# Strassen-like FFN products: the sums of activations move to the middle of the following pair

## What is computed

```
def swiglu_ffn(h, w_up, w_down):
    gate, up = jnp.split(h @ w_up, 2, axis=-1)
    return (jax.nn.silu(gate) * up) @ w_down
...
D_FF = ((8 * D_MODEL // 3 + 127) // 128) * 128
...
x = x + FFN_RESIDUAL_SCALE * swiglu_ffn(h, w_ffn1_up[l], w_ffn1_down[l])
```

## Time and profile before

| | |
|---|---|
| Runs, three | 2237.89, 2242.66, 2243.89 us; median 2242.66 |
| The profiled execution | 2246.15 us, of which the span is 2244.4 |
| PE busy | 2178.8 us, 97% of the span |
| DVE, ACT, POOL busy | 1702.1, 947.4, 625.2 us |
| Granted TensorE clock, mean | 0.991 of full speed |
| First FFN, pairs and down projection | to about 680 us |
| Second FFN, pairs | from about 1600 to 2025 us, then its down projection |

### The profile page before, as it was taken

The page is one execution under the profiler, slowest core; times in us unless marked ns, Lnnn a source line. Parts: engine busy times, 40 slices in busy tenths (PEclk is TensorE's granted clock), DMA queues, the critical chain, the costliest instruction groups (busy, mean ns, idle before and its releaser), DMA issues.

```text
span 2244.4 us, 31503 instructions
## 1 busy us (share of the span) xinstructions
PE 2178.8 (97%) x10238; PEld 1794.4 (80%) x10238; DVE 1702.1 (76%) x2123; ACT 947.4 (42%) x1551; POOL 625.2 (28%) x714
## 2 busy tenths in 40 slices
PE   7999999999999999999999999999989999999997
PEld 6788877878788888888887888888867788888886
DVE  5877878878955999999998659364688876765557
ACT  5455555534455122222224225044355555554444
POOL 2887668999800000000000420000036600000000
PEclk9999999999999999999999999999999999999999
DMA  5235785469874344444544632553258733337764
GB/s 170 78 112 180 255 267 178 154 233 301 267 234 133 100 137 148 147 135 144 151 124 146 209 96 80 187 206 104 75 174 273 265 126 98 112 114 252 234 188 169
DMA packets 306625, 379.07 MB, mean 169 GB/s; under 512 B 27257, under 2 KB 199377, under 8 KB 306416
## 3 DMA queue, kind: packets, MB, share of 16 engines
q1 hardware_dynamic: 286576, 306.01, 43.0%
q0 software_dynamic: 18800, 67.85, 8.8%
q10 hardware_dynamic: 1168, 4.20, 0.5%
HBM read 256.06 MB, written 119.55 MB: 167 GB/s over the span
## 4 chain that ended last, share of the span: by engine, by line
PE 77%; DVE 14%; issue 3%; ACT 3%; DMA 2%; SPq 0%; DVEq 0%; ACTq 0%
PE PU L1392 9%; PE PU L1394 9%; PE PU L1332 9%; PE PU L1393 9%; PE PU L1333 8%; PE PU L1334 8%; PE PD L1267 3%; PE PD L1268 3%; PE PD L1269 3%; PE PU L1267 2%; PE PU L1268 2%; PE PU L1269 2%; DVE Alo L2060 2%; DVE Dlo L2057 2%; PE PD L1468 1%
## 5 line engine op out<-in xcount | busy, mean ns | idle before, releaser
L1332 PE MATMUL PU<-Hhi,Whi 128*128 128x512 f32 x896 | 352.8, 394 | 2.8 <-DVE Hlo L2479 2.7
L1333 PE MATMUL PU<-Hlo,Whi 128*128 128x512 f32 x896 | 349.5, 390 | 0.0
L1334 PE MATMUL PU<-Hhi,Wlo 128*128 128x512 f32 x896 | 349.4, 390 | 0.0
L2458 DVE SCALAR_TENSOR_TENSOR XT<-XT,wq 128x1024 f32<-128x1024 f32 x240 | 313.3, 1306 | 8.2
L1332 PEld LDWEIGHTS PU<-Hhi,Whi 128*128 128x128 f32 x896 | 168.6, 188 | 41.3 <-DVE Hlo L2479 4.0
L1334 PEld LDWEIGHTS PU<-Hhi,Wlo 128*128 128x128 f32 x896 | 168.6, 188 | 35.4
L1333 PEld LDWEIGHTS PU<-Hlo,Whi 128*128 128x128 f32 x896 | 168.5, 188 | 34.8 <-issue 0.7
L1392 PE MATMUL PU<-Hhi,Dhi 128*128 128x512 f32 x480 | 187.0, 389 | 2.2 <-ACT s1b L1734 2.2
L1394 PE MATMUL PU<-Hhi,Dlo 128*128 128x512 f32 x480 | 186.7, 389 | 0.0
L1393 PE MATMUL PU<-Hlo,Dhi 128*128 128x512 f32 x480 | 186.7, 389 | 0.0
L1267 PE MATMUL PD<-Dhi,Ahi 128*128 128x512 f32 x352 | 139.4, 396 | 7.1 <-DVE Alo L2060 7.1
(11 more groups left out here) (400 smaller groups left out, 5195.5 us busy)
## 6 DMA issues: line engine op xcount, KB each, us to landing
TAB<-in_w_ffn_down POOLq DMA_DIRECT2D x44, 512.0 KB, 5.3
d_sb<-TAB POOLq DMA_DIRECT2D x44, 512.0 KB, 4.3
Wraw<-in_w_ffn_up SPq DMA_DIRECT2D x80, 256.0 KB, 4.3
XT<-in_w_ffn_up SPq DMA_DIRECT2D x80, 256.0 KB, 4.0
d_sa<-XT SPq DMA_DIRECT2D x80, 256.0 KB, 2.4
Wraw<-in_w_in SPq DMA_DIRECT2D x32, 512.0 KB, 5.1
d_act<-G SPq DMA_DIRECT2D x48, 256.0 KB, 2.1
WRd<-d_sb SPq DMA_DIRECT2D x44, 256.0 KB, 3.4
```

Source lines behind the costliest of these rows:

```text
L1332: mm(o_, Whi[s][:, side, k, :], Hhi[:, k, hs[h]], start=k == 0, stop=False)
L1333: mm(o_, Whi[s][:, side, k, :], Hlo[:, k, hs[h]], start=False, stop=False)
L1334: last = mm(o_, Wlo[s][:, side, k, :], Hhi[:, k, hs[h]], start=False, stop=k == KT - 1)
L2458: stt(CVb, z_, w_, CVb, ALU.mult, ALU.add).then_inc(m["conv"], 1)
```

## The change

All four halves of a couple now lie in the kept blocks: `K2` and `K3` take the places of `E1` and `E2`, and the odd pair writes ACT1 to K2 and ACT2 to K3. S3 is made in K3 in the middle of the odd pair (before ACT2 goes there), and S1, S2 and S4 in the middle of the even pair that follows, in place: K1, K0, K2. Stores and waits follow: S3 is stored in the odd pair, the other three in the even one behind it, and the product that writes K3 waits for the landing of the store of S3. `comb_s16` and `silu_1` no longer wait for stores of G. Behind the last pair the three sums stand at the steps 4, 5 and 6 of the down projection.

```diff
-    K0, K1, E1, E2 = [XT[:, 6 + i // 2, (i % 2) * HW:(i % 2 + 1) * HW] for i in range(4)]
+    K0, K1, K2, K3 = [XT[:, 6 + i // 2, (i % 2) * HW:(i % 2 + 1) * HW] for i in range(4)]
...
         def store_pair(S, r):
 
             if second(r):
+                store_sums(S, r, (M_S3,))
                 store_kept(S, r, 1)
                 store_kept(S, r, 0)
                 store_sums(S, r, (M_S1, M_S2, M_S4))
             else:
                 store_kept(S, r, 0)
-                store_sums(S, r, (M_S3,))
...
         def comb_s16(S, r, saved1):
             q = pair_at(S, r)[0]
             dve.wait_ge(u_prod, q * 7 + POS[6])
             dve.wait_ge(u_s1, q + 1)
-            if second(r):
+            if isinstance(r, int) and r == 0:
+                dve.wait_ge(act_saved[1], saved1[1] + 32)
+            else:
                 dve.wait_ge(u_c, q * 7 + (C_ACT2 - 7))
-            else:
-                first = isinstance(r, int) and r == 0
-                dve.wait_ge(act_saved[1], saved1[1] + 32 if first else couple(S, r)[0] * 32 + saved1[1])
-                if not first:
-                    dve.wait_ge(u_sum, couple(S, r)[1] * 4)
...
             if second(r):
-                tt(s16b, s16b, s5b, ALU.mult).then_inc(u_c, 1)
-                return
-            dve.wait_ge(t_lo, 4 * (UBASE[S] // NSP) + 4)
-            if S is FFN2 or not isinstance(r, int) or r:
-                dve.wait_ge(sa_st, couple(S, r)[1] * 64)
-            tt(K1, s16b, s5b, ALU.mult).then_inc(u_c, 1)
+                dve.wait_ge(sa_st, couple(S, r)[1] * 64 + 16)
+            else:
+                dve.wait_ge(t_lo, 4 * (UBASE[S] // NSP) + 4)
+                if S is FFN2 or not isinstance(r, int) or r:
+                    dve.wait_ge(sa_st, couple(S, r)[1] * 64)
+            tt(K3 if second(r) else K1, s16b, s5b, ALU.mult).then_inc(u_c, 1)
...
-            tt(g1b if second(r) else K0, g1b, s167b, ALU.mult).then_inc(u_c, 1)
+            tt(K2 if second(r) else K0, g1b, s167b, ALU.mult).then_inc(u_c, 1)
...
+        def sum_3(S, r, saved):
+
+            q, (c, n) = pair_at(S, r)[0], couple(S, r)
+            dve.wait_ge(u_c, q * 7 + (C_ACT1 - 7))
+            dve.wait_ge(act_saved[1], c * 32 + saved[1])
+            tt(K3, K0, K1, ALU.subtract).then_inc(u_sum, 1)
...
+            tt(K1, K1, K3, ALU.add).then_inc(u_sum, 1)
...
+            tt(K0, K1, K0, ALU.subtract).then_inc(u_sum, 1)
...
+            dve.wait_ge(act_saved[1], c * 32 + (saved[1] + 32))
+            tt(K2, K2, K0, ALU.subtract).then_inc(u_sum, 1)
...
                 comb_s16(S, r, saved)
                 lo_w(S, coming, 6)
+                if second(r):
+                    sum_3(S, r, saved)
+                else:
+                    sum_1(S, after(r, -1))
                 comb_12(S, r)
+                if not second(r):
+                    sum_2(S, after(r, -1), saved)
                 lo_w(S, coming, 3)
+                if not second(r):
+                    sum_4(S, after(r, -1), saved)
                 comb_s167(S, r)
                 comb_22(S, r)
                 lo_w(S, coming, 7)
-                if second(r):
-                    sums_high(S, r)
                 comb_21(S, r)
                 lo_w(S, coming, 4)
-                if second(r):
-                    sum_low(S, r, saved)
-                else:
-                    sum_even(S, r)
```

More of the change, by code:

```diff
@@ L524, in store_kept @@
                          else d_act[bass.ds(number(f), 1)].rearrange("a p n -> (a p) n")[:, hs[h]],
-                         G[h][:, :] if second(r) else K0).then_inc(act_saved[second(r)], 16)
+                         (K3 if h else K2) if second(r) else K0).then_inc(act_saved[second(r)], 16)
         def store_sums(S, r, which):
@@ L599, in down @@
                 sp.wait_ge(u_lo, 7 * (UBASE[FFN2] + NSP - 1))
+            r = NSP - 1
             for t in range(RING):
                 load_product(S, 0, t)
-            r = NSP - 1
-            stores = {6: lambda: store_kept(S, r, 1), 7: lambda: store_kept(S, r, 0),
-                      8: lambda: store_sums(S, r, (M_S1, M_S2)), 10: lambda: store_sums(S, r, (M_S4,))}
+            store_sums(S, r, (M_S3,))
+            stores = {(0, 6): lambda: store_kept(S, r, 1), (0, 7): lambda: store_kept(S, r, 0),
+                      (0, 10): lambda: store_sums(S, r, (M_S1, M_S2)), (1, 1): lambda: store_sums(S, r, (M_S4,))}
             for p in range(7):
@@ L608, in down @@
                         load_product(S, p, t)
-                    if p == 0 and t in stores:
-                        stores[t]()
+                    if (p, t) in stores:
+                        stores[p, t]()
                     if (p, t) in D_ROWS_AT:
@@ L1750, in silu_1 @@
             act.wait_ge(u_prod, q * 7 + POS[2])
-            if second(r):
-                act.wait_ge(u_c, q * 7 + (C_ACT1 - 7))
-            elif isinstance(r, int) and r == 0:
+            if isinstance(r, int) and r == 0:
                 act.wait_ge(act_saved[0], saved0[0] + 32)
             else:
-                act.wait_ge(act_saved[1], couple(S, r)[0] * 32 + saved0[1])
-                act.wait_ge(u_sum, couple(S, r)[1] * 4)
+                act.wait_ge(u_c, q * 7 + (C_ACT1 - 7))
             fn(g1b, PUf[0][:, :], ACT.Silu).then_inc(u_g1, 1)
@@ L2287, in comb_21, with sum_1 @@
             dve.wait_ge(u_c, q * 7 + C_21)
-            tt(g1b if second(r) else K0, g1b, s167b, ALU.mult).then_inc(u_c, 1)
[L2290 to L2296, removed]
+            tt(K2 if second(r) else K0, g1b, s167b, ALU.mult).then_inc(u_c, 1)
[4 more added lines that the diff above has]
+            tt(K3, K0, K1, ALU.subtract).then_inc(u_sum, 1)
+        def sum_1(S, r):
             q, n = pair_at(S, r)[0], couple(S, r)[1]
@@ L2300, in sums_high, with sum_2, sum_4 @@
             dve.wait_ge(u_c, q * 7 + C_ACT2)
-            tt(K1, K1, G[1][:, :], ALU.add).then_inc(u_sum, 1)
+            tt(K1, K1, K3, ALU.add).then_inc(u_sum, 1)
+        def sum_2(S, r, saved):
+            c, n = couple(S, r)
             dve.wait_ge(u_sum, n * 4 + M_S1)
-            tt(E2, K1, K0, ALU.subtract).then_inc(u_sum, 1)
-        def sum_low(S, r, saved):
+            dve.wait_ge(act_saved[0], c * 16 + (saved[0] + 32))
+            tt(K0, K1, K0, ALU.subtract).then_inc(u_sum, 1)
+        def sum_4(S, r, saved):
             q, (c, n) = pair_at(S, r)[0], couple(S, r)
@@ L2369, in fast_ffn @@
             lo_w(S, 1, 4)
-            sum_even(S, 0)
             def body(r):
@@ L2426, in _ @@
         fast_ffn(FFN1, 0, 0, SAVED0[FFN1], "nf1")
-        down(FFN1, {(0, 5): lambda: sum_low(FFN1, NSP - 1, SAVED0[FFN1]), (3, 9): lambda: split_pair(R_MIX, 0), (5, 9): lambda: row_scale("nmx", 0),
+        down(FFN1, {(0, 4): lambda: sum_1(FFN1, NSP - 1), (0, 5): lambda: sum_2(FFN1, NSP - 1, SAVED0[FFN1]),
+                    (0, 6): lambda: sum_4(FFN1, NSP - 1, SAVED0[FFN1]), (3, 9): lambda: split_pair(R_MIX, 0), (5, 9): lambda: row_scale("nmx", 0),
                     (6, 9): lambda: turned("nmx", 0, 0), (6, 10): lambda: turned("nmx", 0, 1)})
@@ L2659, in _ @@
         fast_ffn(FFN2, R_FFN2, N1 + 2 * KT, SAVED0[FFN2], "nf2")
-        down(FFN2, {(0, 5): lambda: sum_low(FFN2, NSP - 1, SAVED0[FFN2]), (5, 8): fin_scale, (5, 10): fin_early, (6, 8): fin_half})
+        down(FFN2, {(0, 4): lambda: sum_1(FFN2, NSP - 1), (0, 5): lambda: sum_2(FFN2, NSP - 1, SAVED0[FFN2]),
+                    (0, 6): lambda: sum_4(FFN2, NSP - 1, SAVED0[FFN2]), (5, 8): fin_scale, (5, 10): fin_early, (6, 8): fin_half})
         fin_late()
```

10 lines of the change are left out of this document (4 added, 6 removed).

## The result

| | Before | Changed |
|---|---|---|
| Median, range | 2242.69, 2237.89 to 2243.89 us (4 runs) | 2268.12, 2261.45 to 2276.59 us (4 runs) |
| Profiled execution | 2246.15 us | 2276.59 us, span 2274.8 |

The ratio is 1.0119, 95% interval 1.0080 to 1.0159: slower by 25 us where 12 were forecast. The sign and the range (2226 to 2276) held; the size was half of what came. The profiled execution of the changed kernel is the slowest of its four, 8 us above their median.

A forecast was written before the change was run, and what follows sets the result against it. PE is busy 97% of the span, and in the busy FFN stretches waits only for comb_s16. Terms -24.1, -1.4, -1, +34.8 and +4 sum to +12.3 us: 2255.0 us against the median 2242.66, range 2226 to 2276.

The forecast's parts named there:

- Bound by comb_s16: In both busy FFN stretches PE waits only for comb_s16 to read PU01 before product 7: 8.5 and 6.6 us.
- even stalls from the late sums: All seven even-pair waits come from sums late in DVE's backlog and go when these move: -24.1 us.
- Pair 1, -1.4: Pair 1 of each FFN loses one 0.69 us operation ahead of a late comb_s16: -1.4 us, bounds 0 and -4.
- Junction, -1: At the change to the down projection, sums move within one DVE backlog: -1 us, bounds -3 and +3.
- Quiet couples, 0: In couples without busy POOL traffic, DVE's margin covers the later loads and the K1 wait: 0 us.
- First wait, the loads, 5.8 us in six pairs: Raw-block loads behind the sums' stores land 8.0 us into six busy odd pairs: 5.8 us each, +34.8 together.
- Second wait, "it costs nothing more": Even pair's product into K1 waits for the couple's stores; busy, it ends before the loads land, adding 0 us.
- +4 together: Odd pairs 7, 15 and 17 of FFN1, with POOL computing but few transfers, lose 0 to 4 us each, +4 together.
- Rival 3: Pile-up: last load 2.8 us later, hold_s5 behind the weights' split, 11 us lost in three pairs: 2271, chance 0.18.
- The Trainium skill's price: Store and load price, about 2.0 us fixed plus bytes at 436 GB/s; both waits would end 4 to 5 us earlier.

The follow-up runs named there:

- e4: The kernel before with sum 3 alone, and its store, moved to the middle of the odd pair: 2232.9 us, ratio 0.9964.
- e12: The changed kernel run again without any edit: 2266.6 us, ratio 1.0115.
- e9: The kernel before with one added wait in SP's queue that holds back the loads of the even pair's raw blocks: 2259.8 us, ratio 1.0096.
- e1: The changed kernel with the loads of the even pair's raw blocks ahead of the stores of sums 1, 2 and 4 in SP's queue: 2260.0 us, ratio 1.0093.
- e8: The changed kernel with POOL's loads and stores of the down weights cut to 16 columns, result not valid: 2244.1 us.
- e7: The changed kernel with POOL's subtractions on the down weights cut to 16 of 512 columns, result not valid: 2242.6 us.
- e2: The changed kernel with sum 1 written to K3, the wait for stores moved from the product into K1 to that into K0: 2273.3 us, ratio 1.0108.
- e6: The changed kernel with loads ahead of the sums' stores, sum 1 in K3, and sums 1, 2 and 4 stored one by one: 2218.7 us, ratio 0.9908.

## Why the prediction was right, and what it mis-sized

- **Bound by comb_s16, even stalls from the late sums:** right. Even pairs kept 3.8 of 24.1 us. The forecast of none from pair 8 on was not met: pair 8 of FFN1 lost 1.8, and pair 6 of FFN2 1.9, both behind an odd pair that was itself late.
- **Pair 1, -1.4:** undersized; -5.1, and e4 shows it is sum 3's doing. The stated reason (an operation of 0.69 ahead of a late comb_s16) does not give 2.2 and 2.9 us; I costed the operation and not the slower clock and the chain behind it, though by how much each counts no run tells.
- **Junction, -1:** the 0.0 is luck. PE idles 2.9 us at FFN1's down projection's splits, where it was 4.3, but 3.5 us for comb_s16 of pair 19 (below), and the 156th matmul behind that pair's copy comes 4.3 us later than before. 3.2 of it come back further on in this projection, and the part behind the last copy of FFN2 is 1.9 shorter. In e12 the same matmul comes 5.4 us earlier than before. The term is neither borne out nor refuted.
- **Quiet couples, 0:** right, 38.08 us, the wait on line 2275 of 2.17 us included.
- **First wait, the loads, 5.8 us in six pairs:** the mechanism is there, and its price from the landing on held (e9, and the 4.8 to 6.7 us above). The landing was mis-sized: the last load landed 6.2 to 13.0 us into the six pairs, 9.7 on average, where 8.0 was forecast. The transfers are not what was off (the last load took 7.3 us on average, as in the earlier trace rows); sum 4 was. It ended 14.4 to 19.3 us into the even pair, 16.6 on average, where 14.3 was forecast. This is the term that was most mis-sized, and it feeds both waits: the late landing alone is 1.7 of the 2.5 us by which comb_s16 came later than forecast.
- **Second wait, "it costs nothing more": wrong as a price.** It took a K1 wait that ends 1.1 us into the odd pair, from stores that land in 4.7 us, and the same sum 4 at 14.3. The stores took up to 7.6 us, and the kernel before already had one of 7.1 in this stretch, outside the one couple of the earlier trace rows. In the six pairs the wait ended 0.7 to 7.3 us in, 3.2 on average, and comb_s16 followed 11 to 14 us behind its end, where the prediction's own terms (last split done at 5.4, one split, then its 4.2) give about 9. By itself, with the loads early, this wait cost 30.8 us in the six pairs (e1); beside late loads it was the last to end in one of the six. Together: comb_s16 at 15.9 in place of 13.4, and 7.7 in place of 5.8 us lost.
- **Six couples priced as if each stood alone, and "+4 together" for pairs 7, 15 and 17:** wrong in the same way. A late odd pair starts the next even one with DVE behind, its sums end later, and the next odd pair is later still: 5.5, 8.6 and 5.0, 9.1, 11.4 in a row. Where comb_s16 of the even pair was late, sum 4 ended at 15.7 to 19.3, otherwise at 14.4 to 15.9. Pairs 7, 15 and 17 lost 10.9. Pair 19 lost PE 3.48 us in a way that no term had: line 2275 of pair 18 waited 4.27 us, so the K0 half was stored only at 480.00, and behind that store in SP's queue stand the down projection's first loads, for which ACT, and then DVE's split step ahead of comb_s16, waited. SP, ACT:

```profile
480.00 0.34 SPq L523 DMA_DIRECT2D d_act<-XT  x1
480.39 0.43 SPq L487 DMA_DIRECT2D WRd<-in_w_ffn_down  x1
```

```profile
484.40 0.63 ACT L1625 ACTIVATE Dhi<-WRd 128x512 fp32r<-128x512 f32 x1 [5.21 <-DMA WRd<-in_w_ffn_down]
```

- **Rival 3 (hold_s5 behind the split, 2271)** came nearest in size. Its mechanism cost PE 10.9 us of idling in all, against 32.9 for comb_s16 in the two stretches; in pair 9 of FFN1 the K1 wait feeds it, in pair 5 of FFN2 the late load, as the rival had it (ACT's split at 8.7 us).
- **The Trainium skill's price,** "DMA: Bandwidth & Descriptors", "Anatomy of one DMA", about 2.6 us by an estimate for 256 KB: in e8, with POOL's traffic nearly gone, the stores of FFN2's stretch took 2.0 to 3.0, and the trace agrees with it; in the changed kernel they took up to 7.6. The section is about transfers that GpSimd issues, and its sum of a fixed part and the bytes has no term for other traffic; these are SP's. The prediction's "4 to 5 us earlier" by that price fits the loads alone; the K1 wait would end some 2 us earlier (4.7 less 2.6).
- **DVE's slow sums.** Sums 1, 2 and 4 took 5.5 us in pair 8 against 2.07 in a quiet pair. The Trainium skill says in "GPSIMD Engine Reference", "Specifications", that GpSimd shares its SBUF interfaces with VectorE, with contention for DVE instructions that have two SBUF inputs. The traces agree: operations with a PSUM operand stayed at 0.67 in the same pair, and the sums took 0.69 in FFN2's stretch of e7, where POOL's subtractions were cut to 16 columns, against 1.5 on average in the changed kernel. Three such sums between comb_s16 and comb_s167 are exposed to it as they were at the odd pair's end.

## What to carry to other kernels

When work is moved off a late chain, list everything that is released by it at its new place, and lay the new waits beside each other: two of nearly equal height hide each other, so neither is "nothing more", and an experiment that eases one alone shows little (e1 gave 8 us and e2 nothing, both together 34). Ask the chain of waits which one ended last before naming a cause, pair by pair: here the largest total of waiting was not it. Price a wait in a busy stretch by the spread over the whole stretch, not by one couple, and let a late pair start the next one late. What is worth moving may be one piece of the change (e4), and a store should start when its own data are ready, with loads that wait for nothing ahead of it in the queue (e6).

## What was not expected of the hardware

Three 256 KB stores issued within 1.1 us landed in 2.0, 4.6 and 7.6 us while POOL's 512 KB transfers ran and four loads followed; the DMA share was 0.88 in the window from 259 us on. In quiet time three such stores landed in 2.0 to 2.4 us. Being issued together is not enough: e1 issues the same three together, with no loads right behind, and of its 43 stores of sums in the two stretches none took over 4.1 us:

```profile
DMA to landing us min/median/max: 2.0/2.3/4.1
...
DMA to landing us min/median/max: 2.1/2.3/4.0
```

Issued one by one as their sums were made, they let the changed kernel run 12 us faster and e1 26 us faster, with the same bytes moved.
